# The order of the expert's matrix products on TensorE: down before the next tokens and the combine

## The reference

```
logits = x @ router_w
probs  = softmax(logits)
best group of 4 experts, then the top 2 inside it; wts normalised; comb = their weights
hid = silu(x @ w_gate[e]) * (x @ w_up[e])
out = sum over e of comb[e] * (hid @ w_down[e])
```

## Time and profile before

| | us |
|---|---|
| median of 3 runs | 1003.9 |
| lowest, highest | 1001.24, 1004.36 |
| profiled execution, its own time | 1003.38 |
| its span | 1001.6 |
| PE busy in the span | 902.1 (90%) |
| DVE, ACT, POOL busy | 400.7, 175.7, 217.7 |
| mean granted TensorE clock | 0.946 |
| bytes moved | 277.52 MB |

### The profile page before, as it was taken

The page is one execution under the profiler, slowest core; times in us unless marked ns, Lnnn a source line. Parts: engine busy times, 40 slices in busy tenths (PEclk is TensorE's granted clock), DMA queues, the critical chain, the costliest instruction groups (busy, mean ns, idle before and its releaser), DMA issues.

```text
span 1001.6 us, 12283 instructions
## 1 busy us (share of the span) xinstructions
PE 902.1 (90%) x4936; PEld 490.6 (49%) x4936; DVE 400.7 (40%) x838; ACT 175.7 (18%) x310; POOL 217.7 (22%) x328
## 2 busy tenths in 40 slices
PE   7999988998984799999899879899749999999993
PEld 5888867996343233333333368744233333333331
DVE  4599507726646022122134279602561121221115
ACT  0402140223010111111011153301301111111011
POOL 4579982401021411101010110100211001111000
PEclk8999997999896899999999999999869999999997
DMA  9446739102769579999999936660479789999982
GB/s 269 106 134 256 261 121 306 67 12 98 258 216 408 200 303 409 406 403 401 410 406 425 419 122 198 207 268 0 190 311 368 307 357 406 397 415 398 417 340 87
DMA packets 83579, 277.52 MB, mean 277 GB/s; under 512 B 25337, under 2 KB 44231, under 8 KB 60854
## 3 DMA queue, kind: packets, MB, share of 16 engines
q1 hardware_dynamic: 70298, 255.86, 66.3%
q10 hardware_dynamic: 10660, 16.49, 5.0%
q0 software_dynamic: 2560, 4.33, 1.5%
HBM read 261.49 MB, written 18.01 MB: 279 GB/s over the span
## 4 chain that ended last, share of the span: by engine, by line
PE 73%; DMA 15%; DVE 7%; ACT 2%; issue 1%; SPq 0%; POOL 0%; DVEq 0%; ACTq 0%; POOLq 0%
PE ps L1803 17%; DMA ring<-in_moe_w_up 13%; PE ps L342 11%; PE ps L1827 8%; PE ps L2471 6%; PE ps L1845 4%; PE ps L804 3%; PE ps L1782 3%; PE ps L2333 1%; PE ps L305 1%; PE ps L633 1%; PE ps L1533 1%; PE ps L650 1%; DMA work<-x_rows,work 1%; PE ps L2348 1%
## 5 line engine op out<-in xcount | busy, mean ns | idle before, releaser
L1803 PE MATMUL ps<-ring,work 128*64 128x512 f32 x480 | 217.3, 605 | 11.4 <-DMA ring<-in_moe_w_up 9.9
L1804 PE MATMUL ps<-ring,work 128*64 128x512 f32 x480 | 217.4, 605 | 0.0
L1803 PEld LDWEIGHTS ps<-ring,work 128*64 128x64 f32 x480 | 63.8, 139 | 137.5 <-issue 121.4
L1887 DVE TENSOR_TENSOR work<-ps,work 64x512 f32<-64x512 f32 x32 | 33.8, 1057 | 223.3 <-ACT work L1858 223.3
L342 PE MATMUL ps<-work,ring 128*128 128x264 f32 x512 | 115.2, 387 | 0.0
L1827 PE MATMUL ps<-ring,work 128*64 128x512 f32 x248 | 113.0, 598 | 1.5 <-DVE work L1892 1.4
L1828 PE MATMUL ps<-ring,work 128*64 128x512 f32 x248 | 113.1, 599 | 0.0
L342 PEld LDWEIGHTS ps<-work,ring 128*128 128x128 f32 x512 | 96.8, 190 | 16.4
L1249 POOL TENSOR_TENSOR ring<-ring 128x512 f32<-128x512 f32 (+5 forms) x76 | 90.5, 1207 | 9.5 <-DVE ring L1245 6.2
L1897 DVE COPY work<-ps 64x512 f32<-64x512 f32 x32 | 22.2, 694 | 149.8 <-PE ps L1828 149.8
L1908 POOL COPY work<-work 64x1 int32<-64x1 int32 x32 | 5.7, 178 | 339.6 <-PE ps L1782 300.0
(11 more groups left out here) (491 smaller groups left out, 1187.8 us busy)
## 6 DMA issues: line engine op xcount, KB each, us to landing
ring<-in_moe_w_down SPq DMA_DIRECT2D x31, 2048.0 KB, 17.0
ring<-in_moe_w_gate SPq DMA_DIRECT2D x60, 1024.0 KB, 14.6
ring<-in_moe_w_up SPq DMA_DIRECT2D x60, 1024.0 KB, 16.8
ring<-in_w_in ACTq DMA_DIRECT2D x6, 2048.0 KB, 8.7
s_out_mats<-ring SPq DMA_DIRECT2D x4, 1280.0 KB, 4.7
ring<-in_w_in SPq DMA_DIRECT2D x2, 2048.0 KB, 10.2
s_in_mats<-ring SPq DMA_DIRECT2D x4, 1024.0 KB, 6.3
ring<-in_w_out SPq DMA_DIRECT2D x1, 4096.0 KB, 16.5
```

What stands on the lines that cost most here:

```text
L1803: nc.tensor.matmul(ps[0:SLOT, 5, :], xgT[s][:, c], gate_w[slot][:, c], start=c == 0, stop=c == DC - 1)
L1804: last = nc.tensor.matmul(ps[SLOT:P, 5, :], xgT[s][:, c], up_w[slot][:, c], start=c == 0, stop=c == DC - 1)
L1887: nc.vector.tensor_tensor(hid[s][0:SLOT].rearrange("t (c p) -> t p c", c=4), strided(ps[SLOT:P, 5, :]), strided(sg[s][SLOT:P]), ALU.mult). ...
```

## The change

It permutes four calls in the loop of moe_pe. In iteration k the order becomes gate and up of k, down of k-1, tokens of k+1, the combine (at odd k from 3 on), units of k. No instruction is added or removed, no buffer, wait or load is changed, and the lists of the other engines and of the DMA queues stay as they are. Both layers use the same loop. What follows the loop is the same.

```diff
             for k in range(NE):
                 pe_gate_up(t, l, *at_expert(k))
+                if k > 0:
+                    pe_down(t, l, *at_expert(k - 1))
+                if k + 1 < NE:
+                    pe_tokens(t, l, *at_expert(k + 1))
                 if k % 2 == 1 and k >= 3:
                     pe_combine(t, l, k // 2 - 1, k - 2, slice(0, P), (k // 2 - 1) % 2)
-                if k + 1 < NE:
-                    pe_tokens(t, l, *at_expert(k + 1))
-                if k > 0:
-                    pe_down(t, l, *at_expert(k - 1))
                 pe_units(t, l, *at_expert(k))
             pe_down(t, l, *at_expert(NE - 1))
```

## The result

| | before | after |
|---|---|---|
| median, us (lowest to highest, runs) | 1001.87 (998.06 to 1005.18, 18) | 1005.92 (1002.62 to 1009.34, 18) |
| ratio after / before, 95% interval | | 1.0038 [1.0024, 1.0052] |
| profiled execution: time, span | 1003.38, 1001.6 | 1003.98, 1002.3 |

The change costs 4.05 us (2.4 to 5.2 by the interval), above the 3.0 us that can be told from no change. The forecast was +2.45 on a time before of 1003.9, the median of three runs; over 18, those three among them, it is 1001.87. So 1006 met the measured 1005.92 by luck: the difference was forecast too small by 1.6 us, and the time that it was added to stood 2.0 us too high.

A forecast was written before the change was run, and what follows sets the result against it. Each layer was taken to be bound by its DMA weight stream, with TensorE nearly as long. Layer 0 (-0.9 + 1.0 = +0.1) and layer 1 (+1.3 + 1.05 = +2.35) gave +2.45 on 1003.9, so 1006 us, range 1003 to 1010.5.

The forecast's parts named there:

- What bounds: Both mixture layers: a DMA weight stream that starts late and never pauses after its last hole sets the end.
- The reserve of 6.4 us: Layer 0: TensorE's waits for weights, 6.4 us (3.5 in layer 1), time it can lose without setting the end.
- The test whether TensorE stays inside its reserve: Layer 1's end: gate and up of 15 at 969.4, down's weights at 970.2, so inside by 0.8 us.
- The uncovered wait: Units wait for ScalarE's copy of bank 4, no longer covered by down: 0.75 lost, 0.65 net, 8 times a layer.
- Restart of layer 1: Layer 1's weight stream restarts after its holes 1.3 us later, so all its weights land 1.3 later.
- Earlier downs in layer 0: Layer 0's first down load is issued 0.9 us earlier, moving the whole stream by -0.9.
- The end of a layer: At k = 15 down of 14 newly waits for its weights: last down +1.05 in layer 1, +1.0 in layer 0.
- The sum: Both layers: +0.1 in layer 0 and +2.35 in layer 1, together +2.45, so 1006 us.
- TensorE as the bound: Rival: with a stall of 1.2 TensorE sets the layers' ends, +5.9 and +1.3, together +7.2: 1010.6 us; chance 0.22.
- Copy hidden: Rival: no stall before units (near 0), +1.15, 1004.5 us; chance 0.10.
- holes close: Rival: earlier down loads remove layer 1's stream holes, some 7.9 us: 996.7 us; chance 0.04.
- The clock falls: Rival: each of 16 new waits slows TensorE's clock, +15.1 in layer 1 and +10.5 in layer 0: 1029 us; chance 0.04.

The follow-up runs named there:

- layer0_only: Changed kernel, but with the new order in layer 0 alone and the old order in layer 1: 1005.04 us, ratio to before 1.0040.
- old_at_15: Changed kernel, but in iteration k = 15 of both layers the combine stands ahead of down of 14 again: 1005.79 us, ratio to before 1.0048.
- three_new: Changed kernel, but layer 1's gate/up and down weights rotate through three buffers for all experts: 1003.97 us, ratio to before 1.0005.
- copy_twice: Changed kernel, but ScalarE copies the tokens' bank twice before it signals: 1022.73 us, ratio to before 1.0215.
- bank7: Changed kernel, but units go through bank 7 (down's bank), and ScalarE copies its half of down before the tokens: 1007.97 us, ratio to before 1.0051.
- old_from_10: Changed kernel, but with the old order from iteration 10 on in both layers: 1005.01 us, ratio to before 1.0028.
- gather_late: Kernel before, but with expert 4's gather in layer 0 held back until the units of expert 1 are done: 1002.99 us in one execution.

## Why the prediction came out as it did

- **What bounds.** Right for layer 1. In layer 0 it doesn't always hold once the order is new: in the kernel after the end follows the landing of down 14's weights (by 9.00), in layer0_only, old_at_15 and three_new TensorE sets it. The reserve of 6.4 us was a sum over the layer, and only its last 1.24 (the wait for expert 15's weights) lay behind k = 13, where waits came that the prediction did not have. The test whether TensorE stays inside its reserve was made for layer 1 alone.
- **The uncovered wait.** Right: 0.72 of idle beside 0.75 forecast; net 0.61 each (two waits moved the restart by 1.22) beside 0.65. Eight a layer, none at odd k from 3 on. The releaser shown is "issue", not ScalarE's copy as I had said; the copy's end at 815.49, copy_twice (1.34 each) and bank7 (0.2) say that it is the copy.
- **Restart of layer 1.** Right: +1.22 for 1.3, down to the landing (+1.1). The second hole's restart came 1.06 late, since the combine at k = 3 gave 0.16 back.
- **Earlier downs in layer 0.** The step failed after its first half. The issue was 1.1 earlier, the landings were not: in the new order a gather falls into the stream, and the load takes 8.6 us instead of 7.5. In layer0_only down 14's weights land 0.5 later than before, where -0.9 was forecast; this is the larger part of the miss, 1.4 us. I had called the gathers free, as their data are needed late; that they share the DMA engines with the stream I did not count.
- **The end of a layer.** In layer 1 right: last down 9.0 after the landing of down 14's weights, forecast 8.9, for 7.8 before. In layer 0 the step has the right size in the kernel after (9.00), but it was not the whole of it: layer0_only has 9.55, for 7.87 before, so +1.7 where 1.0 was forecast. The forecast took k = 15 alone, but the queue brings gate/up of k and then down of k-1, exactly TensorE's new order. So down waits at each k where the stream is just behind, from k = 11 on: in the kernel after 2.35, 1.71 and 0.87 at k = 11, 13 and 15, in layer0_only 2.21 and 2.50 at 11 and 13, with slow clock after the second. The old order had combine and tokens (4.2 and 0.9 us) between a landing that gate and up need and the one that down needs. In layer 0 old_from_10 gives all of it back (7.87 again), old_at_15 nothing.
- **The sum.** By segments +2.2 and +2.3, 4.5, for 4.05 measured. The forecast was +0.1 and +2.35: the miss of 2.1 is layer 0's, 1.4 by the stream's head and 0.7 by the end. The time of 1006 fits only because before stood 2 us lower than the three runs said.
- **The rivals.** TensorE as the bound was half true: in layer0_only it sets layer 0's end, though not through a stall of 1.2 but through late waits for down. "Copy hidden" and "holes close" fell with the idles of 0.72 and the restarts at +1.22. "The clock falls" fell for the 16 short waits: the strip has nines over layer 1 (slices 30 to 38, counted from 0), but it returned behind the waits of 2.4 and 2.5 us and in copy_twice.

Two rules of the Trainium skill met the runs. Perfetto Trace Analysis (Matmuls) asks that groups rotate through PSUM banks; the trace agrees for the wait itself (0.72 on one bank, 0.2 in bank7), but no time came back, since the stream took the place of the bank. TensorE: Matmul & The Clock Gate ("A second HAM failure mode: psum-queue depth-cycling") tells of another kernel, whose clock swung through short idles. Here 0.72 in eight iterations of layer 1 left it at 1.00, so the trace doesn't bear it out for idles of this length:

```profile
750.00:975.00 225.00, 215.36 (x1077) 82.57 (x1078) 39.89 (x61) 27.86 (x48) 18.33 (x42) 1.00 0.95 378
```

(the kernel after, all of layer 1's mixture), while the stretch behind a wait of 2.35 us reads 0.77:

```profile
490.00:495.00 5.00, 2.65 (x8) 0.85 (x8) 1.03 (x1) 0.59 (x1) 0.00 (x0) 0.77 1.01 419
```

## What to carry to other kernels

When a consumer's order is made the same as the order of its load queue, the work that used to stand between two landings goes, and waits appear wherever the stream is just behind; look at each iteration's landing, not at the last one's. Price a step that moves other queues' small transfers too: ask whether they ran in a hole. And look for holes in the stream first: a third buffer in one layer brought 0.5%, while none of the orders tried here beat the old one.

## What the runs showed of the hardware

- A gather of 64 rows that falls into a full stream of weights delays the load that it meets by 1.1 us (8.6 instead of 7.5 to landing) and the next ones by 0.7 to 1.1; issued 2.6 us ahead of the load, in a hole, it doesn't.
- Slow clock also comes where no instruction ahead of it was changed. In the kernel after, gate and up of expert 1 in layer 0 ran at half speed for a while (a matmul of 1.06 us instead of 0.59, clock 0.75). This and a longer slow stretch at the layer's start put SP's first down load at t0 + 26.5, in layer0_only at 24.2: 2.3 of the 4.6 in that profile's layer 0. The fall follows, by 0.6 us, an idle of 1.02 before units of 0 that every kernel has in both layers (1.38 in copy_twice); only three of the 13 profiles show a fall behind it (after, old_from_10 and copy_twice).

```profile
339.88 1.06 PE L1803 MATMUL ps<-ring,work 128*64 128x512 f32 x1
...
340.00:345.00 5.00, 5.00 (x20) 1.53 (x18) 0.00 (x1) 0.00 (x0) 0.00 (x0) 0.75 1.02 388
```

- Open: the late lag in gather_late, what the slow clock alone costs late in layer 0, and bank7's one stop of 3.61 us.
